# A 31-tap depthwise convolution in one TensorE-bound kernel: from VectorE and TensorE to all four compute engines

## The reference

```python
def causal_dwconv(x, w, b):
    """Causal depthwise conv over positions. x: (B,S,C), w: (K,C), b: (C,)."""
    ...
def conformer_conv_module(h, w_in, b_in, dw, dw_b, ln_g, ln_b, w_out, b_out):
    u = h @ w_in + b_in
    u = u[..., :D_MODEL] * jax.nn.sigmoid(u[..., D_MODEL:])
    u = causal_dwconv(u, dw, dw_b)
    u = layer_norm(u, ln_g, ln_b)
    u = jax.nn.silu(u)
    return u @ w_out + b_out
```

## Time and profile before

| | us |
|---|---|
| median of three runs (lowest to highest) | 2567.33 (2567.14 to 2568.29) |
| the profiled execution's own time | 2567.04 |
| its span, first to last instruction | 2565.2 |
| TensorE busy | 2408.0 |
| VectorE busy | 725.1 |
| ScalarE busy | 410.0 |
| GpSimd busy | 0.2 |
| convolution taps on VectorE (L1355, 180 of them) | 71.5 |
| convolution on TensorE (L641) | 28.8 |

### The profile page before, as it was taken

How to read it: one execution, slowest core, us unless ns; L and a number is a source line. 1 busy time by engine, 2 the same in 40 slices (tenths; PEclk the granted TensorE clock), 3 DMA queues, 4 the chain that set the end, 5 groups by cost and what they waited for, 6 DMA issues and landing times.

```text
span 2565.2 us, 32855 instructions
## 1 busy us (share of the span) xinstructions
PE 2408.0 (94%) x13468; PEld 1806.2 (70%) x13468; DVE 725.1 (28%) x1780; ACT 410.0 (16%) x928; POOL 0.2 (0%) x4
## 2 busy tenths in 40 slices
PE   8789998999889998999999898999999999999997
PEld 7678887888778887888876587555555555555554
DVE  6722264120432212000344543112111211111112
ACT  4222101000322102000023412111111111111111
POOL 0000000000000000000000000000000000000000
PEclk9899999999999999999999997999999999999999
DMA  6024475664214442132211054899999999999996
GB/s 248 33 99 152 160 276 189 240 226 170 81 66 140 156 148 115 66 115 91 71 70 49 7 211 184 359 422 421 422 422 422 421 422 421 422 421 422 421 422 261
DMA packets 83842, 606.90 MB, mean 237 GB/s; under 512 B 9328, under 2 KB 9712, under 8 KB 10000
## 3 DMA queue, kind: packets, MB, share of 16 engines
q1 hardware_dynamic: 83760, 605.73, 59.8%
HBM read 604.65 MB, written 1.05 MB: 236 GB/s over the span
## 4 chain that ended last, share of the span: by engine, by line
PE 79%; DMA 10%; DVE 7%; ACT 3%; issue 1%; SPq 0%; ACTq 0%; DVEq 0%
PE bank L521 30%; PE bank L898 13%; DMA spare<-in_experts 9%; PE bank L518 8%; PE bank L576 6%; PE bank L925 6%; PE bank L863 3%; PE bank L535 2%; PE bank L892 2%; DVE arena L1355 2%; PE bank L561 2%; PE bank L874 1%; PE bank L641 1%; DVE arena L1240 1%; ACT arena L1148 1%
## 5 line engine op out<-in xcount | busy, mean ns | idle before, releaser
L521 PE MATMUL bank<-arena,ring 128*128 128x256 f32 x3648 | 802.5, 383 | 24.5 <-DVE arena L1246 12.0
L521 PEld LDWEIGHTS bank<-arena,ring 128*128 128x128 f32 x3648 | 701.2, 193 | 124.6 <-issue 27.1
L898 PE MATMUL bank<-ring,arena 128*64 128x256 f32 x2304 | 293.8, 382 | 17.1 <-DMA ring<-in_experts 9.6
L898 PEld LDWEIGHTS bank<-ring,arena 128*64 128x64 f32 x2304 | 175.1, 137 | 130.9 <-DMA ring<-in_experts 19.0
L1703 DVE TENSOR_SCALAR arena<-bank 128x256 f32<-128x256 f32 x64 | 27.2, 425 | 703.6 <-PE bank L898 703.6
L518 PE MATMUL bank<-ring,arena 128*128 128x256 f32 x896 | 196.3, 381 | 0.0
L518 PEld LDWEIGHTS bank<-ring,arena 128*128 128x128 f32 x896 | 171.3, 191 | 23.6
L576 PE MATMUL bank<-arena,ring 128*128 128x256 f32 x704 | 152.3, 379 | 0.0
L576 PEld LDWEIGHTS bank<-arena,ring 128*128 128x128 f32 x704 | 133.8, 190 | 18.2
L1276 DVE SCALAR_TENSOR_TENSOR arena<-bank,par,arena 128x254 f32<-128x254 f32 (+1 forms) x176 | 72.7, 476 | 224.3 <-ACT arena L988 224.3
L898 PE MATMUL bank<-spare,arena 128*64 128x256 f32 x768 | 117.5, 382 | 7.9 <-DMA spare<-in_experts 7.9
(11 more groups left out here) (245 smaller groups left out, 1922.5 us busy)
## 6 DMA issues: line engine op xcount, KB each, us to landing
ring<-in_dense SPq DMA_DIRECT2D x186, 1024.0 KB, 4.8
ring<-in_experts SPq DMA_DIRECT2D x160, 1024.0 KB, 22.1
arena<-in_experts SPq DMA_DIRECT2D x128, 1024.0 KB, 21.4
spare<-in_experts SPq DMA_DIRECT2D x96, 1024.0 KB, 20.4
con<-in_con SPq DMA_DIRECT2D x1, 1248.0 KB, 12.1
X<-in_x SPq DMA_DIRECT2D x1, 1024.0 KB, 4.8
arena<-in_cond SPq DMA_DIRECT2D x1, 1024.0 KB, 17.7
arena<-in_ctx SPq DMA_DIRECT2D x1, 1024.0 KB, 4.8
```

Source lines behind the costliest of these rows:

```text
L521: ins = nc.tensor.matmul(o, w[:, k, j * P:(j + 1) * P], src[:, k, :], start=(k == 0), stop=(k == KT - 1))
L898: ins = nc.tensor.matmul(o, XGT[:, k, e * CAP:(e + 1) * CAP], w[:, k, :], start=False, stop=(k == KT - 1))
```

## The change

The eight chunks are shared among four engines:

- VectorE keeps chunks 0, 1, 4 and 5, and taps 16 to 30 of chunk 6, each tap waiting for the one before (`conv(6, 16, 1)`).
- ScalarE and GpSimd together take chunks 2 and 3 and taps 0 to 15 of chunk 6. ScalarE multiplies a shifted window of G by the tap's weight (`taps`), into one of eight buffers PROD; GpSimd adds the product to the running sum (`sums`). The first tap of a chunk goes straight into the sum, so 78 products need 75 additions. ScalarE waits when it is eight products ahead.
- TensorE keeps chunk 7 alone. Its 31 diagonals are made before unit 0 is read, no longer between the units.
- The gating of all eight chunks moves from VectorE to GpSimd.
- VectorE adds GpSimd's part of chunk 6 to its own, and the bias of chunk 7 as before. The mean's products wait for `conv` or `summed`, by the engine that did the chunk.

`POOL_TAPS` lists the 78 taps in order: ten of chunk 2, then chunks 2 and 3 in turn, then the rest of chunk 3, then chunk 6. `TAPS_AFTER` says how many of them stand, on both engines, ahead of unit j+1: none up to unit 1, then ten more after each unit.

```diff
-        DIAG = tiles(area(NB + 7000, 2 * TAPS * P), 2 * TAPS)
+        DIAG = tiles(area(NB + 7000, TAPS * P), TAPS)
+        PROD = SQ
+        U6 = Y[:, 6, :]
+        POOL_TAPS = [(2, k) for k in range(10)]
+        for k in range(TAPS):
+            POOL_TAPS += [(2, k + 10)] * (k + 10 < TAPS) + [(3, k)]
+        POOL_TAPS += [(6, k) for k in range(16)]
+        TAPS_AFTER = [0, 0, 10, 20, 30, 40, 50, 60, len(POOL_TAPS)]
...
-            for c in (6, 7):
-                pe.wait_ge(sem("glu"), c + 1)
-                for k in range(TAPS):
-                    n = (c - 6) * TAPS + k
-                    pe.wait_ge(sem("diag"), n + 1)
+            pe.wait_ge(sem("glu"), KT)
+            for k in range(TAPS):
+                pe.wait_ge(sem("diag"), k + 1)
...
-            for c in range(KT):
-                pe.wait_ge(sem("conv"), c + 1)
+            for c, done, count in ((0, "conv", 1), (1, "conv", 2), (2, "summed", LAST_SUM[2]), (3, "summed", LAST_SUM[3]),
+                                   (4, "conv", 3), (5, "conv", 4), (6, "conv", 5), (7, "conv", 6)):
+                pe.wait_ge(sem(done), count)
...
+            def taps(first, end):
+                for n in range(first, end):
+                    c, k = POOL_TAPS[n]
...
+                        s = sums_upto(n)
+                        if s > KT:
+                            act.wait_ge(sem("summed"), s - KT)
+                        nc.scalar.activation(PROD[:, s % KT, :], src, ACT.Copy, scale=w).then_inc(sem("tap"), 1)
...
+            pool.wait_ge(sem("pads"), 1)
+            for j in range(8):
+                unit_half(pool, FIRST_UNIT["cm_in"] + j, 2)
+                nc.gpsimd.tensor_tensor(G[:, j, TAPS - 1:], G[:, j, TAPS - 1:], SG[:, j, :], ALU.mult).then_inc(sem("glu"), 1)
+                sums(TAPS_AFTER[j - 1] if j else 0, TAPS_AFTER[j])
+            sums(TAPS_AFTER[7], TAPS_AFTER[8])
...
-            for j in range(8):
-                unit_half(dve, FIRST_UNIT["cm_in"] + j, 2)
-                V.tensor_tensor(G[:, j, TAPS - 1:], G[:, j, TAPS - 1:], SG[:, j, :], ALU.mult).then_inc(sem("glu"), 1)
-                if j in (1, 3, 7):
-                    dve.wait_ge(sem("glu"), j + 1)
-                    conv(min(j - 1, 4))
+            dve.wait_ge(sem("glu"), 2)
+            conv(0)
+            dve.wait_ge(sem("glu"), 6)
+            conv(4)
+            dve.wait_ge(sem("glu"), 7)
+            conv(6, 16, 1)
+            me.ended()
+            dve.wait_ge(sem("summed"), LAST_SUM[6])
+            V.tensor_tensor(U[:, 6, :], U[:, 6, :], U6, ALU.add).then_inc(sem("conv"), 1)
```

More of the change, by code:

```diff
@@ L254, in build, with sums_upto, pool_acc @@
         SG = tiles(area(NB + 15000, 2048), KT)
-        DIAG = tiles(area(NB + 7000, 2 * TAPS * P), 2 * TAPS)
+        DIAG = tiles(area(NB + 7000, TAPS * P), TAPS)
         Y = tiles(area(NB + 4864, 2048), KT)
+        PROD = SQ
[5 more added lines that the diff above has]
+        TAPS_AFTER = [0, 0, 10, 20, 30, 40, 50, 60, len(POOL_TAPS)]
+        def sums_upto(n):
+            return sum(k > 0 for _, k in POOL_TAPS[:n + 1])
+        LAST_SUM = {c: sums_upto(n) for n, (c, _) in enumerate(POOL_TAPS)}
+        def pool_acc(c):
+            return U6 if c == 6 else U[:, c, :]
         F_CA = tiles(area(NB, 512), 2)
@@ L634, in _ @@
             stage("cm_in", H, "n0_h")
[L636 to L642 removed]
+            pe.wait_ge(sem("glu"), KT)
+            for k in range(TAPS):
+                pe.wait_ge(sem("diag"), k + 1)
+                ins = nc.tensor.matmul(banks[WORK + 1][:, 0:T], DIAG[:, k, :], G[:, 7, k:k + T],
+                                       start=(k == 0), stop=(k == TAPS - 1))
             ins.then_inc(sem("conv_pe"), 1)
[L645 to L646 removed]
+            for c, done, count in ((0, "conv", 1), (1, "conv", 2), (2, "summed", LAST_SUM[2]), (3, "summed", LAST_SUM[3]),
+                                   (4, "conv", 3), (5, "conv", 4), (6, "conv", 5), (7, "conv", 6)):
+                pe.wait_ge(sem(done), count)
                 ins = nc.tensor.matmul(banks[WORK][:, 0:T], mean, U[:, c, :], start=(c == 0), stop=(c == KT - 1))
@@ L1025, in _ @@
             act.wait_ge(sem("par_in"), 16)
+            for k in range(TAPS):
+                nc.scalar.activation(DIAG[:, k, :], ident, ACT.Copy, scale=par_col("cm_dw", k * 8 + 7)).then_inc(sem("diag"), 1)
+            def taps(first, end):
+                for n in range(first, end):
+                    c, k = POOL_TAPS[n]
+                    if k == 0:
+                        act.wait_ge(sem("glu"), c + 1)
+                    w, src = par_col("cm_dw", k * 8 + c), G[:, c, k:k + T]
+                    if k == 0 and c < 6:
+                        nc.scalar.activation(pool_acc(c), src, ACT.Identity, bias=par_col("cm_dw_b", c), scale=w)\
+                            .then_inc(sem("tap"), 1)
+                    elif k == 0:
+                        nc.scalar.activation(pool_acc(c), src, ACT.Copy, scale=w).then_inc(sem("tap"), 1)
+                    else:
+                        s = sums_upto(n)
+                        if s > KT:
+                            act.wait_ge(sem("summed"), s - KT)
+                        nc.scalar.activation(PROD[:, s % KT, :], src, ACT.Copy, scale=w).then_inc(sem("tap"), 1)
             for j in range(8):
@@ L1032, in _ @@
                                      bias=par_col("cm_b_in", 8 + j)).then_inc(read_sem(u), 1)
-                for n in range(8 * j, min(8 * j + 8, 2 * TAPS)):
-                    nc.scalar.activation(DIAG[:, n, :], ident, ACT.Copy,
-                                         scale=par_col("cm_dw", n % TAPS * 8 + 6 + n // TAPS)).then_inc(sem("diag"), 1)
+                taps(TAPS_AFTER[j - 1] if j else 0, TAPS_AFTER[j])
+            taps(TAPS_AFTER[7], TAPS_AFTER[8])
             square("ln", lambda c: U[:, c, :], "ln_centred")
@@ L1228, in _, with sums @@
             root("n11", 0)
+        @block.gpsimd
+        def _(pool):
+            def sums(first, end):
+                for n in range(first, end):
+                    c, k = POOL_TAPS[n]
+                    if k == 0:
+                        continue
+                    s = sums_upto(n)
+                    pool.wait_ge(sem("tap"), n + 1)
+                    if k > 1:
+                        pool.wait_ge(sem("summed"), max(sums_upto(i) for i in range(n) if POOL_TAPS[i][0] == c))
+                    nc.gpsimd.tensor_tensor(pool_acc(c), pool_acc(c), PROD[:, s % KT, :], ALU.add).then_inc(sem("summed"), 1)
+            pool.wait_ge(sem("pads"), 1)
[4 more added lines that the diff above has]
+            sums(TAPS_AFTER[7], TAPS_AFTER[8])
         @block.vector
@@ L1343, in _, with conv @@
             normed("n0", rstd("n0", 0), lambda c: ("mix_pre", c))
-            def conv(c):
-                for k in range(TAPS):
-                    for i in range(2):
+            def conv(c, first=0, width=2):
+                for k in range(first, TAPS):
+                    for i in range(width):
                         w, src = par_col("cm_dw", k * 8 + c + i), G[:, c + i, k:k + T]
-                        if k == 0:
+                        if k == first:
                             me.do(V.tensor_scalar(U[:, c + i, :], src, w, par_col("cm_dw_b", c + i),
@@ L1353, in conv @@
                             continue
-                        me.ended(me.n - 1 if k < TAPS - 1 else me.n - 1 + i)
+                        me.ended(me.n - width + 1 if k < TAPS - 1 else me.n - width + 1 + i)
                         ins = V.scalar_tensor_tensor(U[:, c + i, :], src, w, U[:, c + i, :], ALU.mult, ALU.add)
-                        if k < TAPS - 1:
+                        if k < TAPS - 1 or width == 1:
                             me.do(ins)
@@ L1359, in conv @@
                             ins.then_inc(sem("conv"), 1)
-            for j in range(8):
-                unit_half(dve, FIRST_UNIT["cm_in"] + j, 2)
-                V.tensor_tensor(G[:, j, TAPS - 1:], G[:, j, TAPS - 1:], SG[:, j, :], ALU.mult).then_inc(sem("glu"), 1)
-                if j in (1, 3, 7):
-                    dve.wait_ge(sem("glu"), j + 1)
-                    conv(min(j - 1, 4))
+            dve.wait_ge(sem("glu"), 2)
[7 more added lines that the diff above has]
+            V.tensor_tensor(U[:, 6, :], U[:, 6, :], U6, ALU.add).then_inc(sem("conv"), 1)
             dve.wait_ge(sem("conv_pe"), 1)
-            for c in (6, 7):
-                V.tensor_scalar(U[:, c, :], banks[WORK + 1][:, (c - 6) * T:(c - 5) * T], par_col("cm_dw_b", c), None,
-                                ALU.add).then_inc(sem("conv"), 1)
+            V.tensor_scalar(U[:, 7, :], banks[WORK + 1][:, 0:T], par_col("cm_dw_b", 7), None, ALU.add)\
+             .then_inc(sem("conv"), 1)
             dve.wait_ge(sem("ln_mean"), 1)
```

2 lines of the change are left out of this document (1 added, 1 removed).

## The result

The changed kernel takes 2600.81 us (median of four runs, 2599.39 to 2604.82) against 2567.81 for the one before beside it; the ratio is 1.0127, 95% interval 1.0111 to 1.0143. It is 33 us slower, where 22 were predicted. The profiled execution took 2601.82 us, with a span of 2600.0.

The account below looks back on a forecast made before the run. VectorE and TensorE, ending nearly together, were taken to bound the mean's end at 114.07. With the change VectorE ends at 132.6, the mean at 134.0; plus 2.0 for the clock, +21.9 us on 2567.04, so 2589; range 2549 to 2603.

Parts of the forecast that it names:

- What bounds, and that other engines don't touch VectorE's pace: Before the mean, VectorE and TensorE end nearly together; ScalarE and TensorE take nothing from VectorE's 0.396 us per tap.
- ScalarE and TensorE free: In the shared convolution, ScalarE covers its products and TensorE's chunk 7 ends at 87 or 103; neither on the path.
- rival D: ScalarE reads units late, stretching TensorE's `cm_in`; needs over three units (20 us) of lateness; left out, no chance given.
- p, how long GpSimd's instruction lasts: One GpSimd gating or addition in the convolution: 0.43 to 0.85 us, taken as 0.55.
- x, that the two hold each other up: One GpSimd instruction delays VectorE's convolution by nothing up to the whole p; taken as 0.55 us.
- end = 88.0 + 81x: VectorE's convolution ends at 88.0 unhindered, plus x for each of GpSimd's 81 queued instructions: 132.6 with x = 0.55.
- the forecast's side: The hold-up case in the convolution, x from 0.35 to 0.75: slower, 2573 to 2605 us, chance 0.50.
- my 0.95: GpSimd's cycle beside VectorE's taps in the convolution: 0.55 + 0.396 = 0.95 us, so GpSimd is done at 114.
- The clock term: TensorE idles before the last mean products and its clock falls, slowing the sum of squares: 2 us added.
- Rival A: In the convolution VectorE and GpSimd pass each other, p 0.43 to 0.85: faster, -14.8 us at p = 0.7; chance 0.36.

Follow-up runs that it names:

- the memset run: The changed kernel with all 83 of GpSimd's instructions turned into memsets of the same outputs, gating and sums left out: 2551.20 us (one execution).
- copies: The changed kernel with all 83 of GpSimd's instructions turned into copies of their second input, reading one SBUF tensor instead of two: 2574.69 us (one execution).
- gatings alone: The kernel before, with only its eight gatings moved to GpSimd: 2569.9 us, ratio 1.0003.
- the PSUM run: The changed kernel with VectorE's running sums in PSUM, only the last taps of chunks 0, 1, 4, 5 writing SBUF: 2562.89 us, ratio 0.9967 to the kernel before.
- The run with gaps between taps: The changed kernel, but each tap on VectorE waits for the one before it: 2589.37 us (one execution).
- the two runs with gaps: The changed kernel with each GpSimd addition waiting for the one before, 2598.63 us; and with each VectorE tap doing so, 2589.37 us (one execution each).
- spread better: The changed kernel with VectorE's sums in PSUM, GpSimd given 12 taps of chunk 6, interleaved with chunk 3's last ten, nine products per unit: 2555.48 us, ratio 0.9941.
- the earlier gating alone: The kernel before, without GpSimd, with the gatings of chunks 2 to 7 put between VectorE's taps: 2565.16 us, ratio 0.9984.

## Why the prediction was right in sign and too small

**What bounds, and that other engines don't touch VectorE's pace**: right. In the memset run VectorE's 60 taps take 23.83 us beside TensorE, ScalarE and a GpSimd that only writes.

**ScalarE and TensorE free**: right in price, not in every wait. A product of 128 x 256 lasts 0.50 us and follows every 0.40 (nine in 3.68), inside the stated 0.30 to 0.49. TensorE's convolution started at 98.8 rather than 89, and still did not bound. I set aside that ScalarE might read the units late (rival D): ScalarE stood still for 18.9 us, and TensorE's `cm_in` for 4.2 us. That cost nothing by itself, as none of GpSimd's later gatings had to wait for a unit.

**p, how long GpSimd's instruction lasts**: taken as 0.55, and 0.68 where instructions follow one another, 0.87 where they are chained. Both are in the stated range (0.43 to 0.85) or just above. By the Trainium skill, "GPSIMD Engine Reference", section "Performance versus the Vector engine", an eighth of 2048 columns' time was an estimate of 0.56; the measured pace is a fifth above it.

**x, that the two hold each other up**: right, and shown by four runs: sums in PSUM (no hold-up), memsets (none), copies (held), gatings alone (held). The Trainium skill, "SBUF — State Buffer", section "Who interferes with whom", agrees with these as to which instructions collide: two SBUF inputs against a reading GpSimd, not against one that writes. It doesn't agree as to how long. By its words, as I gave them in the prediction, the second is blocked until the first is done; measured were 18.8 us behind 0.48 us taps, and 16.4 us behind 0.72 us additions.

**"Every one of the 81 pushes VectorE's end out by x", end = 88.0 + 81x**: this step failed. I let the two take turns, one instruction each. The runs showed whole stretches in which one engine shut the other out: 18.84 us for one gating behind gapless taps, 16.4 us for one first tap behind gapless additions. VectorE's end, 143.8, is made up like this: 88.0 as predicted; 3.4 for the later start (34.64 for 31.2); 24.7 of waiting for the gating of chunk 5, which I had as hidden behind VectorE's own taps; 17.25 - 0.74 = 16.5 in which it was shut out; 35.06 - 23.75 = 11.3 of taking turns. The last three are 52.5, where 81 x 0.55 = 44.6 was predicted. The remaining 15 taps took 7.7, as predicted. Of the 24.7, 6.6 stand in the PSUM run too, where nobody is held; the other 18.1 are the hold of chunk 2's gating (18.84 - 0.73). The hold-up itself is thus 45.9 us, and that this is so near 44.6 is luck: only 11.3 of it came about by turns, as the formula has it. Two fifths of it are not VectorE being slowed but VectorE being served too well: for 18.8 us it kept GpSimd from the instruction on which ScalarE's products, GpSimd's additions and VectorE's own next pair all depended.

The prediction named as a sign of being wrong that VectorE keeps 0.396 us per tap beside a busy GpSimd. In the first stretch just this happened (60 taps in 23.83 us), and the time still came out on the forecast's side, because the loss had moved into a wait. GpSimd's last addition ended at 122.0, not 114. The run with gaps between taps came out at 2589.4, the number predicted, but that is a coincidence in part: its taps are slower alone by 0.12 us each and its turn, 0.87 us, shorter than my 0.95.

The 3.4 us of late start are not shown to be the change's. The first norm's product took 6.64 us in this execution and 5.10 before; in the run without GpSimd's work (gatings between VectorE's taps) it took 6.36, and the first taps began at 33.78. In the two runs with gaps, which differ from the changed kernel only later, they began at 31.86 and 32.14.

**The clock term**: right. TensorE's granted clock was 0.50 from 120 to 148 us, the lower level of 1.2 GHz, after long idling (columns as in the earlier trace rows):

```profile
116.00:120.00 4.00, 0.00 (x0) 0.00 (x0) 4.00 (x6) 0.00 (x0) 3.32 (x5) 0.93 0.00 0
120.00:124.00 4.00, 0.00 (x0) 0.00 (x0) 4.00 (x8) 0.00 (x0) 1.73 (x3) 0.50 0.00 0
...
144.00:148.00 4.00, 2.76 (x6) 1.77 (x7) 2.23 (x7) 1.16 (x4) 0.00 (x0) 0.50 0.00 0
```

From the mean's end to the next product it is 9.6 us where it was 8.2, 1.4 more, and the last four mean products took 2.09 in place of 1.13 (the memset run), 1.0 more: 2.4 against 2.

**Rival A** (they pass each other) is what the PSUM run makes true, with p at 0.69 and 0.87. It predicted -14.8 us for p = 0.7; measured were about -8 (ratio 0.9967). The mean ended at 103.7 rather than 97.3. Of these 6.4 us, 4.4 are GpSimd's 34 chained additions, which cost 0.18 us more each where I had 0.05; the rest is 1.3 in the tail behind GpSimd and under 1 in its start and its waits for products.

## What to carry to other kernels

In this kernel GpSimd could take elementwise work from VectorE with profit only when VectorE's taps beside it read one tensor from SBUF: with the running sum in PSUM, both engines kept the pace that they have alone. Even so the gain was small, 0.3% and, spread better, 0.6%, where the earlier gating alone gave 0.16%. Where the sum can't be moved, count the cost by dependence, not by turns alone: a dense row of instructions can shut the other engine out for as long as it lasts, so ask what waits for the one shut out. A short instruction that everyone waits for was the worst thing to hand to GpSimd beside a dense stream on VectorE.

## What the runs showed of the hardware that I had not expected

- Exclusion without turns: one 0.73 us gating held for 18.8 us by 60 taps, one 0.41 us first tap held for 16.4 us by GpSimd's additions. A gap of about 0.03 us between VectorE's taps ended the first, one of about 0.14 us between additions the second.
- The limits of that: copies on GpSimd, one per 0.40 us with neither gap nor overlap, did not keep VectorE out (two first taps in 0.91 us, then one tap per 0.51), and one gating begun 0.2 us behind the first of 60 dense taps took 0.85 us.
- The first tap reads only one tensor from SBUF (TENSOR_SCALAR, SBUF to SBUF, float32) and was shut out all the same by additions; with its output in PSUM, it wasn't (two in 0.99 us). Beside memsets two took 0.90 us for 0.73. Which of its accesses collides was not tried apart.
- A float32 tensor of 128 x 256 on GpSimd takes, start to start, 0.68 us to add, and 0.87 where an addition waits for the one before. A copy lasts 0.40 and a memset 0.31; their own pace isn't shown, since ScalarE's products, one per 0.40 us, set it.
- Taps with the sum in PSUM are no slower than with the sum in SBUF: 0.393 us each against 0.396.
